# Orders of the six matmuls of a block and the offsets of the weights' halves in a decoder step on Trainium2

## The reference

```python
def _swiglu(h, w_in, w_out):
    gu = h @ w_in
    gate, up = gu[..., :D_FF], gu[..., D_FF:]
    return (jax.nn.silu(gate) * up) @ w_out

x = x + 0.5 * _swiglu(_rms_norm(x, w['ffn1_norm'][i]), w['ffn1_w_in'][i], w['ffn1_w_out'][i])
```

## Time and profile before

| | |
|---|---|
| median of 3 runs | 2827.66 us (2827.13 to 2836.8) |
| profiled execution | 2834.66 us |
| its span | 2832.9 us |
| granted TensorE clock over the span | 0.99 |
| TensorE busy with matmuls | 2760.7 us (97%) |
| VectorE, ScalarE, GpSimd busy | 1343.1, 952.6, 314.7 us |
| DMA engines' share | 27% |

### The profile page before, as it was taken

How to read it: one execution, slowest core, us unless ns; L and a number is a source line. 1 busy time by engine, 2 the same in 40 slices (tenths; PEclk the granted TensorE clock), 3 DMA queues, 4 the chain that set the end, 5 groups by cost and what they waited for, 6 DMA issues and landing times.

```text
span 2832.9 us, 50103 instructions
## 1 busy us (share of the span) xinstructions
PE 2760.7 (97%) x20853; PEld 2655.2 (94%) x20853; DVE 1343.1 (47%) x1694; ACT 952.6 (34%) x1365; POOL 314.7 (11%) x343
## 2 busy tenths in 40 slices
PE   8999999998999999999999999999999999999998
PEld 7999999997888799999999999999986699999998
DVE  4434347755545554343464344333546754343354
ACT  4222224453333332221242232222337832222243
POOL 2000002301234210000020000000123310000011
PEclk9999999999999999999999999999999999999999
DMA  5222323220001232232231332223212323222231
GB/s 137 74 80 83 89 66 97 75 83 20 18 26 39 77 89 89 74 89 78 75 101 63 112 109 89 79 84 89 74 60 83 128 89 89 87 76 89 76 99 53
DMA packets 308123, 225.71 MB, mean 80 GB/s; under 512 B 8270, under 2 KB 301567, under 8 KB 307967
## 3 DMA queue, kind: packets, MB, share of 16 engines
q1 hardware_dynamic: 307280, 224.26, 26.3%
q0 software_dynamic: 576, 0.00, 0.0%
q10 hardware_dynamic: 162, 0.04, 0.0%
HBM read 212.14 MB, written 12.13 MB: 79 GB/s over the span
## 4 chain that ended last, share of the span: by engine, by line
PE 92%; DVE 4%; ACT 1%; issue 1%; POOL 1%; DMA 0%; DVEq 0%; POOLq 0%; ACTq 0%
PE ps L524 78%; PE ps L1731 2%; PE ps L1680 2%; PE ps L543 1%; PE ps L2334 1%; POOL dx L1020 1%; PE ps L2368 0%; DVE ls L2097 0%; PE ps L1593 0%; DVE w_lo L477 0%; PE ps L1739 0%; PE ps L1507 0%; PE ps L2273 0%; DVE xt L1361 0%; PE ps L2376 0%
## 5 line engine op out<-in xcount | busy, mean ns | idle before, releaser
L524 PE MATMUL ps<-hx_hi,w_lo 128*128 128x320 f32 (+1 forms) x3986 | 1172.8, 294 | 0.0
L524 PE MATMUL ps<-hx_lo,w_hi 128*128 128x320 f32 (+1 forms) x3986 | 1172.2, 294 | 0.0
L524 PE MATMUL ps<-hx_hi,w_hi 128*128 128x320 f32 (+1 forms) x3986 | 1164.8, 292 | 7.5 <-DVE hx_lo L2467 5.5
L462 ACT ACTIVATE w_hi<-raw 128x1024 fp32r<-128x1024 f32 (+1 forms) x362 | 375.8, 1038 | 1223.7 <-PE ps L524 1222.8
L524 PEld LDWEIGHTS ps<-hx_hi,w_hi 128*128 128x128 f32 x3986 | 749.3, 188 | 10.8 <-issue 6.3
L524 PEld LDWEIGHTS ps<-hx_hi,w_lo 128*128 128x128 f32 x3986 | 749.3, 188 | 0.0
L524 PEld LDWEIGHTS ps<-hx_lo,w_hi 128*128 128x128 f32 x3986 | 748.0, 188 | 0.4
L477 DVE TENSOR_TENSOR w_lo<-raw,w_hi 128x1024 fp32r<-128x1024 f32 (+1 forms) x362 | 460.6, 1273 | 109.1 <-ACT w_hi L462 108.9
L524 PE MATMUL ps<-hid_hi,w_hi 128*128 128x320 f32 (+1 forms) x1664 | 492.1, 296 | 3.4 <-DVE hid_lo L1466 2.3
L524 PE MATMUL ps<-hid_lo,w_hi 128*128 128x320 f32 (+1 forms) x1664 | 494.6, 297 | 0.0
L524 PE MATMUL ps<-hid_hi,w_lo 128*128 128x320 f32 (+1 forms) x1664 | 490.1, 295 | 0.0
(11 more groups left out here) (454 smaller groups left out, 2458.9 us busy)
## 6 DMA issues: line engine op xcount, KB each, us to landing
raw<-in_ffn_w_in SPq DMA_DIRECT2D x176, 512.0 KB, 4.9
raw<-in_ffn_w_out SPq DMA_DIRECT2D x64, 512.0 KB, 4.1
raw<-in_a_w_in SPq DMA_DIRECT2D x33, 512.0 KB, 4.6
raw<-in_ffn_w_out SPq DMA_DIRECT2D x32, 384.0 KB, 3.7
raw<-in_ple_w_gate SPq DMA_DIRECT2D x8, 1024.0 KB, 5.1
raw<-in_w_kv SPq DMA_DIRECT2D x16, 512.0 KB, 4.1
k_page<-in_cache_k SPq DMA_DIRECT2D x16, 512.0 KB, 3.3
v_page<-in_cache_v SPq DMA_DIRECT2D x14, 512.0 KB, 4.7
```

Of the source, the lines that this page charges most:

```text
L462: nc.scalar.activation(w_hi[:, m, 0:k], s.view(m, slot), ACT.Copy).then_inc(w_hi_done, 1)
L524: last = nc.tensor.matmul(TILE[m][:, c0:c1], w[:, m, k], h[:, k, c0:c1], start=k == 0 and a == 0, stop=k == k_all - 1 and a == 2)
```

## The change

Each stage has an `order`, by default the old one. Every group of feed-forward products, twelve in all, gets an order of its own, which its gate and up products and its down products share; `multiply` walks through it, and sets the start flag on the first and the stop flag on the last matmul of each part. All other products keep the old order. Independently of that, each half of `w_hi` and `w_lo` gets 8 words (32 bytes) more, so that the four halves begin 4128 bytes after each other; all that is placed behind them moves by 128 bytes.

```diff
+        self.order = "Aw Bw Cw An Bn Cn".split()
...
-        w_hi = whole.take("w_hi", [P, 2, KD, P], F32R)
-        w_lo = whole.take("w_lo", [P, 2, KD, P], F32R)
+        w_hi, w_lo = ([t[:, m, 0:KD * P].rearrange("p (k n) -> p k n", n=P) for m in range(2)] for t in (
+            whole.take("w_hi", [P, 2, KD * P + 8], F32R), whole.take("w_lo", [P, 2, KD * P + 8], F32R)))
...
+        ORDERS = tuple(text.split() for text in (
+            "Cw Aw Bw An Bn Cn", "Bw Aw Cw Bn An Cn", "Aw Cw Bw An Cn Bn",
+            "Aw Bw Cw Cn Bn An", "Aw Bw An Bn Cw Cn", "Aw Bw An Bn Cn Cw",
+            "Cw Bw Aw Cn Bn An", "Aw An Cn Cw Bw Bn", "Bw Cw Aw Bn Cn An",
+            "Bw Bn Aw An Cw Cn", "Cw Bw Aw An Bn Cn", "An Bn Cn Aw Bw Cw"))
...
+                plan[-1 - len(between) * (n == 0)].order = ORDERS[3 * (2 * layer + (name == "ffn2")) + n]
                 product("upd", KD // 2, k, k, pair_loads(w_out, 0, f0, k), HID, coef=0.5,
                         after=after if last else None, sums=last)
+                plan[-1].order = ORDERS[3 * (2 * layer + (name == "ffn2")) + n]
...
+        def firsts(order):
+
+            return {part: min(a for a, x in enumerate(order) if x[1] == part) for part in "wn"}
+
+        def lasts(order):
+
+            return {part: max(a for a, x in enumerate(order) if x[1] == part) for part in "wn"}
...
-                for c0, c1 in PARTS:
-                    for a, (w, h) in enumerate(((w_hi, hi), (w_hi, lo), (w_lo, hi))):
-                        last = nc.tensor.matmul(TILE[m][:, c0:c1], w[:, m, k], h[:, k, c0:c1],
-                                                start=k == 0 and a == 0, stop=k == k_all - 1 and a == 2)
+                factors = {"A": (w_hi, hi), "B": (w_hi, lo), "C": (w_lo, hi)}
+                for a, (name, wide) in enumerate(s.order):
+                    w, h = factors[name]
+                    c0, c1 = PARTS[wide == "n"]
+                    last = nc.tensor.matmul(TILE[m][:, c0:c1], w[m][:, k], h[:, k, c0:c1],
+                                            start=k == 0 and a == firsts(s.order)[wide], stop=k == k_all - 1 and a == lasts(s.order)[wide])
```

More of the change, by code:

```diff
@@ L461, in split_hi @@
                 act.wait_ge(tile_done, unit_no(s, i, r) * 2 + (m - 1))
-            nc.scalar.activation(w_hi[:, m, 0:k], s.view(m, slot), ACT.Copy).then_inc(w_hi_done, 1)
+            nc.scalar.activation(w_hi[m][:, 0:k], s.view(m, slot), ACT.Copy).then_inc(w_hi_done, 1)
             if s.kind == "ple":
@@ L476, in split_lo @@
             dve.wait_ge(w_hi_done, unit_no(s, i, r) * 2 + (m + 1))
-            nc.vector.tensor_tensor(w_lo[:, m, 0:k], s.view(m, slot), w_hi[:, m, 0:k].bitcast(F32),
+            nc.vector.tensor_tensor(w_lo[m][:, 0:k], s.view(m, slot), w_hi[m][:, 0:k].bitcast(F32),
                                     ALU.subtract).then_inc(w_lo_done, 1)
```

## The result

The changed kernel takes 2851.22 us (median of 6 runs, 2845.61 to 2853.53), against 2834.59 for the kernel before in the same number of runs: ratio 1.0061, 95% interval 1.0049 to 1.0072, so slower by 0.6%. On a second occasion it was 1.0069 (1.0055 to 1.0084). The prediction took 2827.66 for the kernel before; its +8.9 us stand against a measured +16.6 here.

What follows compares the result with a forecast made beforehand. The prediction took PE's matmuls, mainly the pace of line 524, as the bound. Offsets +8.9, order 0 and the rest 0 on a median of 2827.66 gave 2836.6 us, with an 8-in-10 range of 2798 to 2860.

Steps and rivals of the forecast that it cites:

- Part 1: Line 524's blocks: new distances from weights to moving tiles cost +10.2 us on hx, -1.3 on hid, +8.9 together.
- 2.6 ns for each step at distance 0: Price per matmul step whose moving tile and weights share an offset modulo 128 B, from three block times.
- one line, so it keeps its offset: Claim that all behind the weights, moved by 128 B, keeps its offset modulo a line of 128 B.
- the third case, p: Line 543's products on p and pw: distance 32 in all six steps, 795 to 800 ns a block.
- Part 2: The twelve orders in line 524's loop: worth 0, as steps at distance 0 over m = 0 and 1 stay equal.
- The sign named for it: If the twelve groups spread by over 10 ns a block, order matters in itself.
- -7 us for split runs of narrow steps: Possible gain if a narrow step behind a wide one saves 10 ns; four orders, 720 blocks; kept outside the sum.
- Part 3: Counts of matmuls, columns and weight loads, flags, splits and waits: no effect, 0 us.
- A: Rival: nothing couples the two reads, hid is slower for another reason, neither part does anything; 2827.7 us, chance 0.10.
- B: Rival, slower: once w_lo and w_hi differ, every block costs 0.80 us; +30 us, 2857.5 us, chance 0.26.
- C: Rival, faster: w_hi and w_lo at one offset cause the cost, four offsets save 9.3 ns a block; -26 us, chance 0.22.
- the forecast case: The prediction's main outcome: +1 to +14 us, 2829 to 2842 us, chance 0.42.

Runs made afterwards that it cites:

- the shift by 64: Kernel before, old order, with everything placed behind w_lo moved by 64 B: 2843.64 us in one run.
- w_lo at 64: Kernel before, old order, with both halves of w_lo moved to offset 64 and all behind by 128 B: ratio 0.9969, median 2824.06 us.
- a shift by 128 B alone: Kernel before, old order, with everything placed behind w_lo moved by 128 B: 2850.82 us in one run.
- the shift by 256: Kernel before, old order, with everything placed behind w_lo moved by 256 B: 2835.20 us in one run.

## Why the prediction was right or wrong

**The bound: right.** Only the steps of line 524 moved; PE stayed busy, and the waits on w_lo stayed at nothing (0.2 us).

**Part 1, offsets: right in size, wrong in its reason.** Forecast +10.2 on hx and -1.3 on hid, +8.9 together; measured alone +10.4 and -3.0, +7.4 by blocks (+3 by the median, for the reason given with the result). On hx it met the tiles too: 787 for m = 0 and 797 for m = 1, and "stages whose order did not change are slower too" was seen in qkv, kv and q. On hid it had 797 for m = 0 and 792 for m = 1, and they were 787 and 798. The price "2.6 ns for each step at distance 0" had been drawn from three cases, and that it gave the right size on hx was luck: the shift by 64 and w_lo at 64 give 793 and 787 on hid where the count says 787 and 797. The step "one line, so it keeps its offset" failed as well (793 in place of 787 for a shift by 128 B alone). If distances count in 256 B, as the shift by 256 suggests, the third case, p, was also misplaced: it lies 160 B from its weights, not 32. What held is the idea under it, that the place of the moving tiles relative to the weights changes the block time; that it is the weights loaded beside each step, one by one, is not shown.

**Part 2, order: the step that failed.** "By the same count it is worth nothing." The count adds up six steps, whatever goes before each. Measured, the orders alone cost +6.0 us by blocks, +7.0 on hx and -1.0 on hid, and on top of the new offsets 15.1 - 7.4 = +7.7 us. This is most of what the sum was short by: +8.9 forecast, +15.1 by blocks, +16.6 measured. The sign named for it came: alone, the groups on hx spread from 787 to 800 ns, and in the changed kernel those on hid from 791 to 805. The rows had a hint: An and Cn, narrow steps with the same moving tile and both at distance 0, had 0.11 and 0.12. I used it for the rival and not for the sum. The -7 us for split runs of narrow steps had no basis either: I had counted four orders with more than one narrow run, but "Aw Bw An Bn Cn Cw" has a single one, and of the three that remain two are at 800 on hx, the dearest, and "Bw Bn Aw An Cw Cn", with three runs, is at 793.

**Part 3: right.** The splits stayed hidden: line 543 waits 0.2 us for w_lo.

**The rivals.** A, no coupling (2827.7), fell with the shift by 64 B. The Trainium skill (TensorE: Matmul & The Clock Gate, "Step-by-step: what each phase is for") says that loading the next weights takes no read bandwidth from the running matmul; as a rule for the time of this kernel's blocks that does not hold, since moving w_lo alone changed a block by 6 to 9 ns. Whether it is bandwidth that is lost, the runs don't show. B, all blocks at 800, overshot: the change has 795 and 794. But half of its +30 us came, and its point of decision, +5 ns a block (+14 us), was just passed: by blocks +15.1. C, four offsets free every block, fell as it stood, since no stage went below 786. Its idea that w_hi and w_lo at one offset cost something is not refuted for hid, where w_lo at 64 gained 9 ns; on hx equal offsets already have the 787.

**The numbers.** 2851.22 lies in the range of 2798 to 2860, though the range owes that to B; the forecast case's own range, +1 to +14 us, was missed, by +15.1 by blocks as by +16.6. Of the 14.6 us between 2836.6 and 2851.22, 6.9 are the kernel before, whose median went from 2827.66 to 2834.59 with six runs. Most of the chance, 0.52, was on a difference within 0.5%; it was 0.6%, slower.

## What to carry to other kernels

When PE is busy throughout and still slower than its columns, read the starts of its matmuls, not their durations: a pace that repeats to the nanosecond in every stage and differs between two tiles of the same shape was here a matter of addresses and sequence. Then change one distance, look at one short stage, and keep what gives the lowest pace for each pair of tiles; here two gaps of 64 bytes, or one other order on one pair, gave 0.3 to 0.4%, while scattering orders and offsets lost 0.6%. A price for each single step does not add up across such a loop: try the whole sequence.

## What the runs showed of the hardware

- The time of a block of 1728 columns at a granted clock of 1.00 was between 787 and 807 ns in the mean of each stage, in all kernels, by the distances between moving and weights tiles (moved by 32 to 128 B) and by the sequence of the six matmuls. Neither the stage nor the layer moved it by more than 1 ns: at the old offsets and in the old order hx had 786.6 to 787.6 in each.
- Where it stayed put from block to block it was 786.7, 793.3, 800.0 and 806.7 ns: steps of 6.67 ns, which is 16 cycles of 2.4 GHz. Hid at the old offsets doesn't stay put: by the starts in the trace its blocks take 791, 796, 800, 796 and 797 ns, over and over, which is 796.0 in the mean and looks like 0.79 and 0.80 in the earlier trace rows. Why it goes in such steps, and why 786.7 was never undercut, is open.
- Distances counted the same after 256 B more, not after 64 or 128 B more. This was tried for one set of offsets.
- That the two reads meet in the memory is an inference. The runs show that the place of w_lo relative to the other tiles matters, and not where the time is lost inside a step.
